# Two transformer blocks on one Trainium2 core: memory projections from raw weights, a convolution divided anew, and norm factors applied behind a projection

## The reference, cut to what matters

```python
def hybrid_layer(x, mem, ...):                      # first block
    h = rmsnorm(x, norm_mix_g)
    q, k, v, qi, ki, wi, glu = jnp.split(h @ w_in, cuts, axis=-1)
    a_out = dsa_attention(q, k, v, qi, ki, wi)      # 8 heads of 64, 256 keys chosen per query
    ga, gg = jnp.split(glu, 2, axis=-1)
    u = ga * jax.nn.sigmoid(gg)                     # 512 channels
    u = causal_dwconv(u, conv_b_w, conv_b_b)        # 31 taps per channel
    b_out = jax.nn.silu(layernorm(u, ln_b_g, ln_b_b))
    x = x + jnp.concatenate([a_out, b_out], axis=-1) @ w_out
    hq = rmsnorm(x, norm_cross_g)
    m = rmsnorm(mem, norm_mem_g)                    # 256 memory tokens of width 1024
    qc = hq @ w_q_cross
    kc = m @ w_k_cross
    vc = m @ w_v_cross
    ...                                             # cross attention, then the FFN (width 2816)

def second_block(x, ...):
    ...                                             # y_lru, y_att: 512 channels each
    y = jnp.concatenate([rms_norm(y_lru, norm_lru_out[l]),
                         rms_norm(y_att, norm_att_out[l])], axis=-1)
    x = x + jnp.einsum('bse,ed->bsd', y, w_out[l])
    ...                                             # FFN, final norm
```

## Time and profile before

| what | value |
|---|---|
| median of 3 runs | 1419.82 us (1416.19 to 1422.59) |
| the profiled execution | 1419.84 us, of which the span from first to last instruction is 1418.0 us |
| busy PE | 1367.1 us, 96% |
| busy weight loads (beside PE) | 1096.9 us, 77% |
| busy DVE | 780.3 us, 55% |
| busy POOL | 606.4 us, 43% |
| busy ACT | 539.2 us, 38% |
| mean granted clock of PE | 0.983 of full speed |
| DMA | 121.20 MB, 85 GB/s over the span |

### The profile page before, as it was taken

The page is one execution under the profiler, slowest core; times in us unless marked ns, Lnnn a source line. Parts: engine busy times, 40 slices in busy tenths (PEclk is TensorE's granted clock), DMA queues, the critical chain, the costliest instruction groups (busy, mean ns, idle before and its releaser), DMA issues.

```text
span 1418.0 us, 18066 instructions
## 1 busy us (share of the span) xinstructions
PE 1367.1 (96%) x6240; PEld 1096.9 (77%) x6240; DVE 780.3 (55%) x1091; ACT 539.2 (38%) x843; POOL 606.4 (43%) x295
## 2 busy tenths in 40 slices
PE   7999898999999999999999999999999999999997
PEld 5687776887777888888888777666778888888885
DVE  6698995253446777777523588655453333332222
ACT  4454667253333232223223353534342322323321
POOL 3487981342134444444444433122244444444341
PEclk8999999999999999999999999999999999999998
DMA  6122320121122232223322222111123232223321
GB/s 220 45 90 82 112 75 31 60 89 60 60 74 90 92 101 92 101 95 114 102 87 91 89 75 74 45 45 45 45 89 100 92 100 92 103 94 103 101 91 71
DMA packets 31876, 121.20 MB, mean 85 GB/s; under 512 B 3536, under 2 KB 3664, under 8 KB 31568
## 3 DMA queue, kind: packets, MB, share of 16 engines
q1 hardware_dynamic: 31392, 119.55, 25.0%
q10 hardware_dynamic: 432, 0.96, 0.3%
HBM read 118.40 MB, written 2.10 MB: 85 GB/s over the span
## 4 chain that ended last, share of the span: by engine, by line
PE 74%; issue 13%; POOL 5%; DVE 4%; ACT 2%; DMA 1%; POOLq 0%; SPq 0%; DVEq 0%; ACTq 0%
PE acc L1615 60%; POOL weights_low L584 3%; PE acc L1753 3%; POOL conv L633 2%; PE aux L1985 1%; PE aux L2005 1%; PE acc L1725 1%; PE aux L1987 1%; DVE aux L1154 1%; PE aux L1839 1%; PE aux L1820 1%; DVE a_low L1310 1%; DMA weights_raw<-w 1%; PE aux L1809 1%; PE aux L1995 1%
## 5 line engine op out<-in xcount | busy, mean ns | idle before, releaser
L584 POOL TENSOR_TENSOR weights_low<-weights_raw,weights_high 128x1024 fp32r<-128x1024 f32 (+1 forms) x204 | 524.6, 2572 | 781.9 <-ACT weights_high L661 778.9
L661 ACT CAST weights_high<-weights_raw 128x1024 fp32r<-128x1024 f32 (+1 forms) x202 | 221.8, 1098 | 511.3 <-PE acc L1615 478.8
L1615 PE MATMUL acc<-a_high,weights_high 128*128 128x512 f32 x976 | 390.0, 400 | 4.5 <-POOL weights_low L584 3.1
L1615 PE MATMUL acc<-a_high,weights_low 128*128 128x512 f32 x976 | 381.2, 391 | 0.0
L1615 PE MATMUL acc<-a_low,weights_high 128*128 128x512 f32 x976 | 380.8, 390 | 0.0
L1615 PEld LDWEIGHTS acc<-a_high,weights_high 128*128 128x128 f32 x976 | 183.9, 188 | 47.0 <-issue 6.3
L1615 PEld LDWEIGHTS acc<-a_low,weights_high 128*128 128x128 f32 x976 | 184.0, 189 | 39.5 <-issue 2.6
L1615 PEld LDWEIGHTS acc<-a_high,weights_low 128*128 128x128 f32 x976 | 183.8, 188 | 38.9
L1127 DVE TENSOR_TENSOR residual<-acc,residual 128x512 f32<-128x512 f32 (+1 forms) x64 | 44.0, 687 | 197.4 <-PE acc L1615 140.0
L1615 PE MATMUL acc<-h_high,weights_high 128*128 128x512 f32 x352 | 137.6, 391 | 0.0
L1615 PE MATMUL acc<-h_high,weights_low 128*128 128x512 f32 x352 | 137.0, 389 | 0.0
(11 more groups left out here) (347 smaller groups left out, 1920.2 us busy)
## 6 DMA issues: line engine op xcount, KB each, us to landing
weights_raw<-w SPq DMA_DIRECT2D x172, 512.0 KB, 3.2
weights_raw<-w SPq DMA_DIRECT2D x32, 704.0 KB, 4.0
residual<-xT SPq DMA_DIRECT2D x8, 256.0 KB, 7.2
out<-y_tok SPq DMA_DIRECT2D x4, 512.0 KB, 3.7
mem_raw<-memT SPq DMA_DIRECT2D x1, 1024.0 KB, 5.4
mem_tok<-mem SPq DMA_DIRECT2D x1, 1024.0 KB, 7.4
lru_weights<-blockdiag ACTq DMA_DIRECT2D x1, 512.0 KB, 3.4
sine<-positions ACTq DMA_DIRECT2D x1, 256.0 KB, 7.0
```

What stands on the lines that cost most here:

```text
L584: g.tensor_tensor(weights_low[:, s, 0:cols], weights_raw[:, s, 0:cols], weights_high[:, s, 0:cols].bitcast(F32), ALU.subtract).then_inc(we ...
L661: a.copy(weights_high[:, s, 0:cols], weights_raw[:, s, 0:cols]).then_inc(weight_high, 1)
L1615: last = t_.matmul(acc[:, bank, 0:cols], w[:, s, wide], x_[:, k0 + k, 0:cols], start=start and k == opens and n == 0, stop=stop and k == c ...
```

## The change

1. **Memory projections.** `m_high`, `m_low` and the splitting of the 16 chunks `kc` and `vc` are gone. PE multiplies `weights_raw` by the scaled memory `m_raw`, both plain f32, one product for each pair of blocks in place of three passes; the profile shows an f32 product as two matmul records. ACT's and POOL's ends of these chunks issue nothing, except that the ends of chunks 30 and 31 (memory chunks 14 and 15) convert and split chunks 32 and 33, the first of the out projection. SP loads chunks of the stretch when `chunk_done` says that PE has finished with the buffer. `weight_high` and `weight_low` count 17 at once at chunk 32, so that later counts stay as they were. `mem_scale` goes from POOL to ACT. The first masking on DVE waits for `mem_root` in place of `mem_low`.
2. **Convolution.** Blocks 0 and 1 (62 products, 60 adds) go to ACT and POOL; blocks 2 and 3 (62 taps) stay on DVE. The taps are spread over 21 steps (before 25), the products over 22 (before 24). `mean` stands at step 23, `variance` at 24, `ln_spread` at 26, `ln_low` at 27.
3. **Norm factors of the second mixer.** `lru_scale` and `att_scale` are gone. ACT makes `y_high` from value times gain, DVE `y_low` from value times gain minus `y_high`, as soon as a block of the operand is there. The token factors are copied as rows to `xc[:, 1]` and `xc[:, 2]`. Every finished half tile is first multiplied by that row in PSUM, then added to the residual (`normed_residual`), for both kinds. The last block of the attention is taken from `aux[4]` without its copy to `q2`. The eight halves of kind 0 stand one to a step from 24 and two to a step from 32; the first pieces of kind 1 (`last`) stand around `att_sum` and `att_spread`.

The diff, cut to what these three parts do:

```diff
-        SHARED_TAPS = 9
-        PRODUCTS = [(1, k) for k in range(SHARED_TAPS)] + [(0, k) for k in range(TAPS)]
-        CONV = [(n, k) for n in (2, 3) for k in range(TAPS)] + [(1, k) for k in range(SHARED_TAPS, TAPS)]
+        PRODUCTS = [(n, k) for n in range(2) for k in range(TAPS)]
+        CONV = [(n, k) for n in (2, 3) for k in range(TAPS)]
...
-        CONV_STEPS, PRODUCT_STEPS = 25, 24
+        CONV_STEPS, PRODUCT_STEPS = 21, 22
...
-            if step == 25:
+            if step == 23:
                 FIRST_PLAN.append(("mean",))
+            if step == 24:
+                FIRST_PLAN.append(("variance",))
             if step == 26:
-                FIRST_PLAN.append(("variance",))
-            if step == 28:
                 FIRST_PLAN.append(("ln_spread",))
-            if step == 29:
+            if step == 27:
                 FIRST_PLAN.append(("ln_low",))
...
-            if step < 34:
-                REC_PLAN.append(halves.pop(0))
-        REC_PLAN += [("att_square", 3)] + halves[:2] + [("att_sum",)] + halves[2:3]
-        REC_PLAN += [("att_spread",)] + halves[3:4] + [("att_scale",)] + halves[4:]
+            REC_PLAN += halves[:1 + (step >= 32)]
+            halves = halves[1 + (step >= 32):]
+        REC_PLAN += [("att_square", 3), ("last", 0, 0), ("last", 1, 0), ("att_sum",), ("last", 0, 1),
+                     ("last", 1, 1), ("att_spread",), ("last", 0, 2), ("last", 1, 2), ("att_row",)]
...
-            with sp.Fori(2, CHUNK["down"] // 2) as m:
-                for s in range(2):
-                    load(m, s, w8_chunk(2 * m + s), KB * P)
+            for first, end, used in ((2, CHUNK["kc"] // 2 + 1, weight_low),
+                                     (CHUNK["kc"] // 2 + 1, CHUNK["out"] // 2 + 1, chunk_done),
+                                     (CHUNK["out"] // 2 + 1, CHUNK["down"] // 2, weight_low)):
+                with sp.Fori(first, end) as m:
+                    for s in range(2):
+                        load(m, s, w8_chunk(2 * m + s), KB * P, used)
...
+            def high_after(q):
+
+                if not CHUNK["kc"] <= q + 2 < CHUNK["out"]:
+                    high(q // 2 + 1, q % 2, count=splits(q + 2))
...
             def fill_ends(n):
 
                 q = CHUNK["kc"] + n
-                high_next(q // 2, q % 2)
+                high_after(q)
...
-                elif what == "mem_high":
+                elif what == "mem_scale":
+                    act.wait_ge(memT_in, 16)
                     for k in range(*n):
-                        act.wait_ge(mem_scaled, k + 1)
-                        a.copy(m_high[:, k], mem_raw[:, k]).then_inc(mem_high, 1)
+                        a.activation(m_raw[:, k], m_raw[:, k], ACT.Copy, scale=col("g_mem", k)
+                                     ).then_inc(mem_scaled, 1)
...
+            def normed_residual(s, n, t, row):
+
+                own.then(v.tensor_tensor(acc[:, s], acc[:, s], row, ALU.mult))
+                add_residual(s, n, t)
...
-                    add_residual(n[1], 2 * j + n[1], TILE["out2"] // 2 + j)
+                    normed_residual(n[1], 2 * j + n[1], TILE["out2"] // 2 + j, xc[:, 1])
...
-                elif what == "lru_scale":
-                    scale_parts(RT["ylru"], lru_gate, "g_lru")
+                elif what == "lru_row":
+                    dve.wait_ge(factor_spread, RT["ylru"] + 1)
+                    v.tensor_copy(xc[:, 1], aux[5][:]).then_inc(row_copied, 1)
...
+                    low_of(q2[:, j] if j < 3 else aux[4][:], 4 + j, col("g_att", j), OP["yatt"] + j + 1)
...
-                chunk(q // 2, q % 2, end, q % 2, M, cols=MB * P, first=k)
+                    for i in range(k, end):
+                        last = t_.matmul(acc[:, n % 2, 0:MB * P], weights_raw[:, q % 2, i * P:(i + 1) * P],
+                                         m_raw[:, i], start=i == 0, stop=i == KB - 1)
...
-                pe.wait_ge(weight_low, q + 1)
                 i = k // 4
                 for b in range(MB):
-                    rows, wide = slice(b * P, (b + 1) * P), slice(i * T, (i + 1) * T)
-                    for p_, (w, x_) in enumerate(((weights_high, m_high), (weights_high, m_low),
-                                                  (weights_low, m_high))):
+                    last = t_.matmul(acc[:, b], m_raw[:, 2 * part + i, b * P:(b + 1) * P],
+                                     weights_raw[:, q % 2, i * T:(i + 1) * T], start=part == 0 and i == 0,
+                                     stop=part == 3 and i == 1)
```

143 lines of the change are left out of this document (66 added, 77 removed).

## The result

The changed kernel takes 1436.63 us (median of 4 runs, 1433.17 to 1441.37), the kernel before 1421.2 us in the same comparison. The ratio is 1.0128, with a 95% interval from 1.0103 to 1.0153: 1.3% slower, 15 us at the medians. The prediction was 1426.3 us with a range of 1413 to 1436; the time lies just outside it and the loss is over twice the one forecast.

What follows compares the result with a forecast made beforehand. VectorE was taken to set the pace up to the first mixer's mean, a PE and ScalarE relay the tail. +5.8 us for parts 1 to 3 and +0.7 for the norm factors gave +6.5 on 1419.84: 1426.3 us, range 1413 to 1436.

Steps and rivals of the forecast that it cites:

- Part 1: Memory projections: raw-weight halves of 1.74 us, +11 us of PE in all; memory scaling adds 0.7 us to the path.
- Part 2: First mixer's convolution: GpSimd's adds at 95% use let the mean begin at 212, 6.4 us sooner; ends 208 and 217.
- Part 3: Tail from mean to out projection: 47.0 us against 34.8, +12.2; out projection at 259.0, +5.8 for parts 1 to 3.
- my own five terms: Tail from mean to chunk 30's end: mean 3.7, step 24 3.65, variance 3.7, step 25 3.3, logits and half 2.6; M+16.7.
- Part 4: Last out projection, norm factors: -5.1 us up to the second kind, +5.8 over eight tiles bound by VectorE; sum +0.7.
- Rival 1: Convolution: GpSimd and ScalarE hinder each other, GpSimd 85% used, mean at 220.5, 1435 us; chance 0.24 together with rival 2.
- rival 2: Last out projection: PE's clock falls between the eight tiles, a low-clock tile 5.1 us, 1435 us; 0.24 together with Rival 1.
- Rival 3: Tail: new waits covered, loads land while ScalarE is occupied anyway, mean at 208; -4 and -5.5, 1417 us; chance 0.14.

Runs made afterwards that it cites:

- e1: The kernel before with only the memory projections from raw weights, convolution and second mixer as before: 1414.18 us, ratio 0.9969.
- e5: The changed kernel with mean, variance, ln_spread and ln_low back at steps 25, 26, 28 and 29: 1421.25 us, ratio 1.0006 to before.
- e13: The changed kernel with four product buffers instead of two, the mean still at step 23: 1437.12 us, one run.
- e4: The changed kernel with chunks 32 and 33 loaded early into two buffers of their own: 1428.49 us, ratio 1.0073 to before.
- e7: The changed kernel with ScalarE's conversions of chunks 32 and 33 later, behind the silus and the copy of step 29: 1422.04 us, one run.
- e2: The kernel before with only the new convolution division and the mean two steps sooner, memory projections in three passes: 1453.92 us, ratio 1.0253.
- e3: The kernel before with only the norm factors moved behind the second mixer's projection: 1419.04 us, ratio 0.9999.
- e10: e5 with four product buffers instead of two: 1412.60 us, one run.

## Why the prediction was wrong

One sentence ahead of the prediction has to be put right first: the out projection of the first mixer takes the convolution's half of its operand first, and the attention's half second (`half_tile` is called with blocks 4 to 7 first). The prediction does not use the sentence, but the place of the silus ahead of the out projection follows from it.

**Part 1.** Right in its prices (1.72 us a half, 0.6 us of PE's wait for the scores at the scaling of the memory, loads of 3.5 to 3.7 us), wrong in calling its gain "only in part 2". Alone it brings the mean 5.5 us sooner. I had taken the pace of the steps from VectorE's busy share, 80.8 of 87.4 us, and asked nothing of the 11.9 us in which PE was idle beside it. Of these 5.6 were waits for GpSimd's low parts and 1.9 for `vc`; in e1 PE is idle for 4.2 of 82.0 us. That these waits set the pace, and not something else that went with them, is argued from this, not tested by itself.

**Part 2.** 213.9 for a forecast of 212: near. GpSimd's first add began at 136.55 (137.5 forecast), at 1.41 us each (1.38), with 5.8 us of gaps where I took 3.7. VectorE's load came out at 63.7 us, which is 80.8 less 17, where I had written 61. But since part 1 alone gives a mean at 213.0 with two more steps done by then, the new division gained nothing and cost the two steps; with these at their old place and two buffers (e5) the mean is 5.8 us later than in e1. I compared with the kernel before only, never with the parts of the change one by one.

**Part 3 is the step that failed.** Forecast 47.0 us, measured 53.0. The waits were where I had put them and of the size I gave: 1.84 (1.9), 5.44 (5.5), 3.51 (4). What was mis-sized is the work between them. From the copy behind the silus to the end of chunk 31 I had 7.4 us, measured 11.6 (247.22 to 258.86), because PE works at the lower of its clocks there: the granted clock is 0.68 from 248.1 to 266.9 us and 0.79 over the tail, 0.86 over that of before. This term repeats: from chunk 30's end to the out projection e13 takes 33.9 us and the changed kernel 34.5, for a forecast of 30.3. Another 1.7 us lie ahead of chunk 30's end (18.4 us after the mean, not 16.7; my own five terms add up to 16.95): the variance takes 4.1 us instead of 3.7, the step after it 3.7 instead of 3.3, the logits and the half behind it 3.6 instead of 2.6. This part does not repeat: the same stretch takes 16.8 us in e4 and in e7, and 20.1 in e13, where PE had waited 2.80 us ahead of the mean. The low clock goes on into the out projection, whose first six passes stand 0.43 us apart: 13.9 us of shift at its start have become 16.1 at chunk 34. I charged for waits, and the clock behind them only in the three steps that showed it before.

In the sum: mean 2 us late, tail forecast 6 too short, clock behind it 2, together 10 of the 16.1 us for which I had 5.8. Of the profiled 21.6 us, 0.7 are the norm factors', 3.1 are spells of low clock behind the first mixer and 1.8 lie in the final stage. The medians differ by 15.4, so an ordinary execution of the changed kernel has less of all this than the profiled one; how much less in the tail isn't on record.

**Part 4.** Near in the sum (+0.7 in the profiles; alone it is 0.9999 by the medians), in part by luck. The gain of 5.4 us up to the second kind holds the low clock of the kernel before (clock 0.74 from 1012 to 1025 us). That clock is not part of every execution. e2 has the same instructions there and the same wait, and PE goes on at full speed (0.50 us for the first pass, 0.79 in the earlier trace rows), which makes the stretch 2.5 us shorter; e1 lies between (0.9 us shorter):

```profile
1049.60 0.50 PE L1748 MATMUL acc<-y_high,weights_high 128*128 128x512 f32 x1 [2.87 <-DVE residual L1126]
```

Against such an execution the norm factors would gain 2.9 us there, not 5.4. On the other side the tiles cost 4.4 to 4.5 us in e3, e5 and e10, and the changed kernel's +6.1 holds 1.6 us of low clock (0.87 from 1028 to 1041 us, 1.00 where e10 does the same work). A tile is 0.51 us longer, not 0.72. The reason was half right: I took VectorE's busy time as the bound of the tiles, and it is the chain from the add over ScalarE's high part to the low part.

**Rivals.** The time is that of rivals 1 and 2 (1435), by neither mechanism. Rival 1 had the mean at 220.5; it was at 213.9, though the hindrance it names is real: ScalarE's waits for adds rose from 6.5 to 16.3 us, and four buffers brought them to 6.7. The clock held between the residual tiles (rival 2): it is 1.00 from 1041 to 1067 us. Rival 3, that the landings lie beside work that waits anyway, is what happens in e1 and e5: it needs the variance and the silus behind the ends of the chunks, and the change moved just these. To find it I would have had to walk the tail once with the old order and once with the new.

## What to carry to other kernels

Before a step is moved in a fixed order, look at what is waiting beside it: a long piece of work may be the cover of a load or of a queue that blocks, and a wait in PE's timeline can cost its own length and then the clock of what follows. Where one engine makes pieces and another uses them, try a third and fourth buffer before you divide the work anew (6 to 9 us at the mean here, for 4 KB per partition). When a change has parts, price each part alone against the kernel before; of the three here one gained 0.3%, one nothing that can be measured, and the third lost 2.5% alone and about 1.6% beside the others, all of which could be had back.
